# A three-layer block on one core: who issues the DMAs that turn an SWA pair's weights

## The chip, the cores and the metric

The kernel runs on one core of one Trainium2 chip. The metric is the device time in microseconds, the median of several executions. All data is 32-bit float; a product of two matrices is made of three TensorE products of high and low parts (see below).

## The reference, cut to what matters

The input x is 512 tokens of 2048 features. It passes an MLA attention layer, a sliding-window attention layer (SWA) and a third layer (stick-breaking attention and a gated recurrence), each with a projection in, a mixer, a gate and a projection out. The change touches the SWA layer:

```python
q, k, v, gate = split(rmsnorm(x) @ w_in)         # 32 query heads, 4 key/value heads, head size 64
q, k = rope(q), rope(k)                          # on the first 16 of 64 features
s = q_block @ k_window.T * 64 ** -0.5            # 128-query blocks, 256 keys (block before, own block)
s = where(0 <= query - key < 128, s, -1e30)
m = max(max(s), sink)
p = exp(s - m) / (sum(exp(s - m)) + exp(sink - m))
y = p @ v_window
x = x + (y * silu(gate)) @ w_out
```

## The kernel before, in words

The core's five engines run one instruction stream each: TensorE (the functions that end in `_T`), ScalarE (`_A`), VectorE (`_V`), GpSimd (`_G`) and SyncE (`sync_program` and the `_dmas` functions). They meet by semaphores: `q.did("turned")` counts a step up, `q.at("V.turned")` is the count to wait for. The order of every stream is written out by hand; there is no planner.

Every weight tile is 2048 x 128, loaded by SyncE into one of two `raw` buffers (1 MB) and treated in four pieces of 512 columns. ScalarE makes the high part of a piece (`hi`, line 604: a copy to fp32r), VectorE the low part (`lo`, line 612: the rest), TensorE does 4 x 3 matmuls on it (`multiply`, lines 638 to 640).

The SWA layer is a loop over 16 pairs of heads. Body i projects pair i (query tile, then gate tile, 48 matmuls each) and does the attention of pair i-1. Bodies 1 to 15 do both (`attn and proj`); body 16 has no projection and begins the output projection instead. In one body:

- TensorE: the scores of pair i-1 (16 matmuls, lines 1931 and 1932), the query tile's four pieces, the product of probabilities and values of pair i-2 (`pv_prev`, lines 1960 and 1962), the gate tile's four pieces.
- VectorE: `maxima` of the scores, the inverse sums, the low part of the gathered weights of pair i-2, then `turn_pair` for both heads (line 1898, a transpose inside 32 x 32 blocks, into `turned`; after the second one V.turned counts up). Then the rotary step on q (lines 2219 to 2224), the third low part of the gate tile, `q_lo0` and `q_lo1`, which wait for ScalarE's `q_hi0` and `q_hi1`, the gate tile's fourth low part, the sums for pair i-2 (line 2189), two elementwise steps, and the four low parts of the next query tile. The next body begins with the eviction of the gate (line 2180) and the maxima.
- ScalarE: the exponentials (line 2039), the normalisation (line 2060) with the gate tile's first and second high parts after one head each, a tanh, the third high part, `low_prev` (two copies out of PSUM, line 2067), the fourth high part, `q_hi0` and `q_hi1`, three high parts of the next query tile, `gathered_hi` (the high part of the gathered weights, 128 x 1792), and the fourth high part of the next query tile.
- SyncE: the loads of the next weight tiles, and after V.turned the 16 DMAs from `turned` to `gathered` (line 1161). These move 32 x 32 blocks between partition groups, 4 groups by 4 (QUADS = 4), and so finish the transpose that VectorE began. The next load of a weight tile stands behind them.

`gather_dmas(q, run, bands)` issues a DMA for each of the four destination column bands and each partition band in `bands`. Two constants, `SYNC_BANDS, SCALAR_BANDS = ((0, 1), (2, 3))` (line 46), halve the partition bands. In the MLA stage and in the third layer SyncE issues the first half and ScalarE the second; in the SWA stage SyncE issues all 16. `gathered_hi` waits for the semaphores of all DMAs of the pair, whoever issues them (lines 2071 and 2072).

Of the kernel before, what the change touches and what calls it, by code (L numbers as in the profile page):

```python
# [44 lines left out]
QUADS = P // Q32  # L45
SYNC_BANDS, SCALAR_BANDS = ((0, 1), (2, 3))
# [3 lines left out]
PAIR_SLOTS = 2 * 7 * Q32  # L50
# [316 lines left out]
def build(nc, x, positions, sinks, params, consts, w, out):  # L367
# [6 lines left out]
    with ExitStack() as ctx:  # L374
# [191 lines left out]
        def load_tile(eng, tile):  # L566
            if tile.has(RAW):
                eng.wait_ge(s_lo, tile.raw_free())
            for dst, src, s in weight_dmas(tile):
                eng.dma_start(dst, src).then_inc(s, 16)  # L570
# [20 lines left out]
        def hi(q, tile, p):  # L591

            if tile.at < 2:
                q.eng.wait_ge(s_first[tile.at][p], 16)
            elif p == 0:
                q.eng.wait_ge(s_raw[tile.slot], tile.loaded())
                if tile.phase == "mla" and tile.k == 1:
                    q.eng.wait_ge(s_ukv, lin(32, 32, tile.i))
            if tile.has(SPLIT // PIECES):
                q.eng.wait_ge(s_used, tile.slot_free(p))  # L600
            dst = split(w_hi, tile, p)
            if stacked(tile, p):
                dst = dst[:, :, 0:ROPE1]
            q.eng.activation(dst, raw_piece(tile, p), ACT.Copy).then_inc(s_hi, tile.ups(p))  # L604
# [60 lines left out]
        def loop(eng, a, b, step=1):  # L665
            return eng.Fori(a, b, step)
# [61 lines left out]
        def store_y(q, phase, body, tile_at):  # L728

            q.eng.wait_ge(*q.at("V.y" if phase == "mla" else "V.y_prev", body=body, phase=phase))  # L730
            q.eng.dma_start(y_dram[tile_at], (y_out if phase == "mla" else s_y)[:, 0, :]).then_inc(s_ystore, 16)

        def load_y(q, n, part):

            attention, units, last = BEFORE[n]
            stores = sum(BEFORE[m][1] - 1 for m in range(1, n)) + (4 * part + 4 if n < 3 and part < 3 else units - 1)
            q.eng.wait_ge(s_ystore, 16 + 16 * stores)
            q.eng.wait_ge(s_used, Tile(attention, units - 1, last).used(part))
            chunks = slice(4 * part, min(4 * part + 4, KC - 2 if n == 2 else KC - 1))
            q.eng.dma_start(y_whole[:, chunks, :], y_dram[chunks].rearrange("c p s -> p c s")).then_inc(s_yload[part], 16)  # L740

        def attention_dmas(q, phase, n):
            units, tiles = PHASES[phase][1:]

            def gather(i):
                q.eng.wait_ge(*q.at("V.turned", body=i, phase=phase))
                if phase == "mla":
                    gather_dmas(q, SLOTS, SYNC_BANDS)
                else:
                    gather_dmas(q, PAIR_SLOTS, range(QUADS))  # L750

            def unit(i, store, odd=None, turned=True):
                for k in range(tiles):
                    load_tile(q.eng, Tile(phase, i, k, odd))
                    if k == 0 and turned:
                        gather(i - 1)
                if store:
                    store_y(q, phase, i - 1, i - (2 if phase == "mla" else 3))
            unit(0, False, turned=False)
            unit(1, False, turned=False)  # L760
            if phase == "mla":
                with loop(q.eng, 2, units - 1, 2) as i:
                    unit(i, True, False)
                    unit(i + 1, True, True)
            else:
                unit(2, False)
                with loop(q.eng, 3, units) as i:
                    unit(i, True)
            load_tile(q.eng, Tile(f"out{n}", 0, 0))
            gather(units - 1)  # L770
            if phase == "mla":
                load_tile(q.eng, Tile(f"out{n}", 0, 1))
                for part in range(3):
                    load_y(q, n, part)
                store_y(q, phase, units - 1, units - 2)
            else:
                store_y(q, phase, units - 1, units - 3)
                q.eng.sem_inc(s_ystore, 16)
                load_y(q, n, 2)
            if n == 1:  # L780
                q.eng.wait_ge(*q.at("V.qn_lo", body=units - 1, phase=phase))
                q.eng.dma_start(s_pos_i, positions.to_broadcast([P, S])).then_inc(s_pos, 16)
                q.eng.wait_ge(*q.at("T.s0", body=units, phase=phase))
                q.eng.dma_start(s_sinks[:, 0, :], sinks.to_broadcast([P, H2])).then_inc(s_pos, 16)
# [371 lines left out]
        def gather_dmas(q, run, bands):  # L1156

            for half in range(2):
                for a in (2 * half, 2 * half + 1):
                    for k in bands:  # L1160
                        q.eng.dma_start(gathered[k * Q32:(k + 1) * Q32, a * run:(a + 1) * run],  # L1161
                                        turned[a * Q32:(a + 1) * Q32, k * run:(k + 1) * run]).then_inc(s_turned[half], 16)
# [860 lines left out]
        def swa_A(q, i, proj, attn, nxt):  # L2023
# [3 lines left out]
            def this_hi(p):  # L2027
                if proj:
                    hi(q, Tile("swa", i, 1), p)
# [33 lines left out]
            def low_prev(half):  # L2063

                if attn and (not isinstance(i, int) or i >= 2):
                    q.eng.wait_ge(*q.at(f"T.pv_prev{half}"))
                    q.eng.activation(s_y_low[0:HD2, half, :], PAIR_BANK[half][HD2:P, :], ACT.Copy).then_inc(*q.did(f"low_prev{half}"))
# [26 lines left out]
            if attn:  # L2094
                q.eng.wait_ge(*q.at("V.gate"))
                q.eng.activation(s_th[:, :], s_gate, ACT.Tanh, scale=0.5).then_inc(*q.did("tanh"))
            this_hi(2)
            low_prev(0)
            low_prev(1)
            this_hi(3)  # L2100
# [717 lines left out]
        @block.scalar  # L2818
        def _(eng):
            q = Program(eng, "A", sems, steps)  # L2820
            load_A(q)
            in_A(q)
            in_pairs(q, mla_A, Tile("out1", 0, 0))
            y_hi(q, 1, range(12, KC))
            output_A(q, 1)
            norm2_A(q)
            kv_A(q)
            pipelined(q, swa_A, "swa", Tile("out2", 0, 0))
            y_hi(q, 2, range(KC - 1, KC))
            output_A(q, 2)  # L2830
            norm3_A(q)
            pipelined(q, stick_A, "stick", Tile("out3", 0, 0))
            y_hi(q, 3, range(KC - 1, KC))
            output_A(q, 3)
# [75 lines left out]
```

## Time and profile before

| | |
|---|---|
| median of three runs | 2108.74 us (2108.37 to 2108.83) |
| the profiled execution | 2110.29 us, its span 2108.5 us |
| TensorE busy | 2089.3 us, 99% |
| VectorE busy | 1413.6 us, 67% |
| ScalarE busy | 995.6 us, 47% |
| granted TensorE clock, mean | 0.997 of full speed |
| the SWA loop, first score matmul of body 1 to that of body 16 | 771.19 to 1152.01 us |

Times in the profile are microseconds from the span's start. A group of instructions is named by line, engine, operation and "output<-input". An engine's busy share is an average over stages; in each stage only the wait that ends last counts. SPq, ACTq and DVEq are the instruction sequencers of SyncE, ScalarE and VectorE. A row's idle time in brackets is that of the engine before the row, and behind the arrow stands what ended it. Matmuls are pipelined, so the start of one to the start of the next (0.23 us for 512 columns) is what a matmul costs TensorE.

### The profile page before, as it was taken

To read this page: it belongs to the slowest core of one execution; us is meant where nothing else is said; L and a number is where in the kernel's file an instruction comes from. 1 tells how busy PE (TensorE), PEld (TensorE's weight loads), DVE (VectorE), ACT (ScalarE), POOL (GpSimd) and SP (SyncE) were. 2 spreads that over 40 slices of the span, in tenths; PEclk is the share of its full clock that TensorE was granted. 3 is DMA by queue.
4 is the path that set the end of the run, shared out by engine and by line. 5 is a ranking of instruction groups with operands and counts; after the bars stand their busy time and mean duration, and the time that the engine had idled before them with its cause. 6 is when DMAs were issued, how large, how long until landed. Compare 5 with 4: busy or idle time off the path is not lost. (4 is left out here: it accounts for less than half of the span.)

```text
span 2108.5 us, 30019 instructions
## 1 busy us (share of the span) xinstructions
PE 2089.3 (99%) x9716; PEld 1740.0 (83%) x9716; DVE 1413.6 (67%) x2575; ACT 995.6 (47%) x1925; POOL 191.5 (9%) x197
## 2 busy tenths in 40 slices
PE   9999999999999999999999899999999999999999
PEld 7888888888888888888887688888888888888887
DVE  6677777777633567888888533777777676769432
ACT  6444444444423446666666533544454545446221
POOL 0101111113101000100000122200000000003000
PEclk9999999999999999999999899999999999999999
DMA  7324444446634524444445534533434334345742
GB/s 231 95 80 115 115 113 110 109 110 184 191 80 123 169 72 122 127 126 132 132 133 159 176 100 118 168 104 80 118 92 134 82 103 114 103 114 155 214 115 70
DMA packets 405033, 262.88 MB, mean 125 GB/s; under 512 B 18928, under 2 KB 378096, under 8 KB 404976
## 3 DMA queue, kind: packets, MB, share of 16 engines
q1 hardware_dynamic: 393120, 251.27, 42.2%
q10 hardware_dynamic: 11856, 10.89, 1.9%
q8 instruction: 31, 0.51, 0.1%
q14 instruction: 26, 0.21, 0.0%
HBM read 210.07 MB, written 23.86 MB: 111 GB/s over the span
## 5 line engine op out<-in xcount | busy, mean ns | idle before, releaser
L638 PE MATMUL pp<-act_hi,w_hi 128*128 128x512 f32 x2304 | 905.4, 393 | 7.7 <-POOL act_lo L1545 3.3
L640 PE MATMUL pp<-act_hi,w_lo 128*128 128x512 f32 x2304 | 899.7, 390 | 0.0
L639 PE MATMUL pp<-act_lo,w_hi 128*128 128x512 f32 x2304 | 899.4, 390 | 0.0
L612 DVE TENSOR_TENSOR w_lo<-raw,w_hi 128x512 fp32r<-128x512 f32 x680 | 455.1, 701 | 357.9 <-ACT w_hi L604 357.0
L604 ACT ACTIVATE w_hi<-raw 128x512 fp32r<-128x512 f32 (+1 forms) x684 | 396.0, 622 | 460.8 <-PE pp L640 223.5
L638 PEld LDWEIGHTS pp<-act_hi,w_hi 128*128 128x128 f32 x2304 | 434.2, 188 | 101.5 <-DVE w_lo L612 6.5
L640 PEld LDWEIGHTS pp<-act_hi,w_lo 128*128 128x128 f32 x2304 | 433.8, 188 | 91.6
L639 PEld LDWEIGHTS pp<-act_lo,w_hi 128*128 128x128 f32 x2304 | 434.3, 189 | 87.0 <-issue 0.2
L657 POOL TENSOR_TENSOR pT_lo<-gathered,pT_hi 128x640 fp32r<-128x640 f32 x30 | 46.5, 1570 | 358.8 <-ACT pT_hi L653 358.8
L1314 ACT ACTIVATE prob<-ps,minus,q_scale 128x512 f32<-128x512 f32 (+1 forms) x64 | 39.0, 615 | 78.3 <-DVE minus L1394 78.3
L638 PE MATMUL ps<-act_hi,w_hi 128*128 128x512 f32 x176 | 69.3, 394 | 0.0
L640 PE MATMUL ps<-act_hi,w_lo 128*128 128x512 f32 x176 | 68.5, 389 | 0.0
L639 PE MATMUL ps<-act_lo,w_hi 128*128 128x512 f32 x176 | 68.5, 389 | 0.0
L2039 ACT ACTIVATE s_prob<-ps,s_minus 128x256 f32<-128x256 f32 x96 | 44.6, 471 | 42.7 <-DVE s_minus L2154 42.7
L1702 POOL TENSOR_TENSOR acc<-acc,square 128x512 f32<-128x512 f32 x30 | 41.1, 1371 | 252.6 <-ACT square L1628 251.8
L1545 POOL TENSOR_TENSOR act_lo<-y_lru,act_hi 128x512 fp32r<-128x512 f32 x7 | 11.1, 1619 | 560.5 <-ACT act_hi L1535 560.5
L653 ACT ACTIVATE s_pT_hi<-gathered 128x1792 fp32r<-128x1792 f32 x15 | 25.5, 1702 | 71.2 <-DMA gathered<-turned 71.2
L2060 ACT ACTIVATE s_prob<-s_prob,s_inv 128x256 f32<-128x256 f32 x128 | 54.3, 503 | 0.0
L2154 DVE CUSTOM_DVE_ANT_0 ps<-ps,s_con,s_sink 128x256 f32<-128x256 f32 x96 | 47.4, 549 | 3.2 <-DVEq L2151 3.2
L1898 DVE STREAM_TRANSPOSE turned<-s_prob 128x128 f32<-128x128 f32 (+1 forms) x60 | 35.1, 624 | 12.4 <-ACT s_prob L2060 12.4
L1679 DVE TENSOR_TENSOR xT<-pp,xT 128x512 f32 (+1 forms) x28 | 19.3, 689 | 32.1 <-PE pp L640 32.1
L639 PEld LDWEIGHTS ps<-act_lo,w_hi 128*128 128x128 f32 x176 | 33.0, 188 | 7.3 <-issue 0.5
(432 smaller groups left out, 2753.9 us busy)
## 6 DMA issues: line engine op xcount, KB each, us to landing
raw<-w_in SPq DMA_DIRECT2D x48, 1024.0 KB, 6.0
raw<-swa_w_in SPq DMA_DIRECT2D x36, 1024.0 KB, 5.9
raw<-mla_w_in SPq DMA_DIRECT2D x23, 1024.0 KB, 5.8
raw<-mla_w_out SPq DMA_DIRECT2D x16, 1024.0 KB, 6.8
raw<-w_out SPq DMA_DIRECT2D x16, 1024.0 KB, 6.8
raw<-swa_w_out SPq DMA_DIRECT2D x15, 1024.0 KB, 6.5
gathered<-turned SPq DMA_DIRECT2D x240, 56.0 KB, 2.0
x_feature_major<-xT SPq DMA_DIRECT2D x8, 1024.0 KB, 9.7
```

What stands on the lines that cost most here:

```text
L604: q.eng.activation(dst, raw_piece(tile, p), ACT.Copy).then_inc(s_hi, tile.ups(p))
L612: q.eng.tensor_tensor(dst, raw_piece(tile, p), high, ALU.subtract).then_inc(s_lo, tile.ups(p))
L638: q.eng.matmul(psum[:, :], wh, ah, start=start and n == 0, stop=False)
L639: q.eng.matmul(psum[:, :], wh, al, start=False, stop=False)
L640: last = q.eng.matmul(psum[:, :], wl, ah, start=False, stop=stop and n == PIECE // P - 1)
L657: q.eng.tensor_tensor(out, in_, hi_part.bitcast(F32), ALU.subtract).then_inc(*q.did(step))
L1314: q.eng.activation(prob[:, OFF[b]:OFF[b] + w_], SCORE[b][:, 0:w_], ACT.Exp, bias=minus[:, b:b + 1], scale=q_scale[:, b:b + 1], accum_out=t ...
L1702: q.eng.tensor_tensor(into, into, src[:, k, :], ALU.add).then_inc(*q.did(f"sum{f}{k}"))
L1898: m = q.eng.transpose(out_, in_)
L2039: q.eng.activation(s_prob[:, h, b * 2 * P:(b + 1) * 2 * P], BANKS[h][half][:, b % 2 * 2 * P:(b % 2 + 1) * 2 * P], ACT.Exp, bias=s_minus[:, ...
L2060: m = q.eng.activation(pr, pr, ACT.Identity, scale=s_inv[:, h, b:b + 1])
L2154: m = q.eng.tensor_tensor_reduce(scores, scores, sc("band")[:, b * 2 * P - half * 2 * P:(b + 1) * 2 * P - half * 2 * P], s_q_scale[:, b:b ...
```

## The change

SyncE issues eight of a pair's sixteen gather DMAs, those of partition bands 0 and 1. ScalarE waits for V.turned after the gate tile's third high part and issues the other eight, of bands 2 and 3. Nothing else is changed; the count that `gathered_hi` waits for is the same.

```diff
@@ attention_dmas (SyncE), gather(i) @@
                 if phase == "mla":
                     gather_dmas(q, SLOTS, SYNC_BANDS)
                 else:
-                    gather_dmas(q, PAIR_SLOTS, range(QUADS))
+                    gather_dmas(q, PAIR_SLOTS, SYNC_BANDS)
@@ swa_A (ScalarE) @@
                 q.eng.wait_ge(*q.at("V.gate"))
                 q.eng.activation(s_th[:, :], s_gate, ACT.Tanh, scale=0.5).then_inc(*q.did("tanh"))
             this_hi(2)
+            if attn and proj:
+                q.eng.wait_ge(*q.at("V.turned"))
+                gather_dmas(q, PAIR_SLOTS, SCALAR_BANDS)
             low_prev(0)
             low_prev(1)
             this_hi(3)
```

## Rows read from the trace of the kernel before

**Rows 1.** The page, busy time of each engine.
```profile
PE 2089.3 (99%) x9716; PEld 1740.0 (83%) x9716; DVE 1413.6 (67%) x2575; ACT 995.6 (47%) x1925; POOL 191.5 (9%) x197
```

**Rows 2.** Timeline of TensorE: start, duration, what; first score matmuls of bodies.
```profile
771.19 0.28 PE L1931 MATMUL ps<-pairk_hi,s_q_a 128*128 128x256 f32 x1
...
794.66 0.39 PE L640 MATMUL pp<-act_hi,w_lo 128*128 128x512 f32 x1
794.89 0.28 PE L1931 MATMUL ps<-pairk_hi,s_q_a 128*128 128x256 f32 x1
...
820.28 0.28 PE L1931 MATMUL ps<-pairk_hi,s_q_a 128*128 128x256 f32 x1
...
1126.30 0.28 PE L1931 MATMUL ps<-pairk_hi,s_q_a 128*128 128x256 f32 x1
...
1152.01 0.28 PE L1931 MATMUL ps<-pairk_hi,s_q_a 128*128 128x256 f32 x1
```

**Rows 3.** Waits: total, times, longest; weight loads 995 to 1145, TensorE 760 to 1210.
```profile
PEld pp L638 <- DVE w_lo L612: 1.6, 6, 0.3
...
PE pt L1943 <- DVE y_whole L2239: 3.7, 1, 3.7
```

**Rows 4.** Timeline of SyncE's issues, bodies 2 and 14.
```profile
808.57 10.02 SPq L1161 DMA_DIRECT2D gathered<-turned  x16
...
1116.78 10.03 SPq L1161 DMA_DIRECT2D gathered<-turned  x16
```

**Rows 5.** Timeline of ScalarE, body 14.
```profile
1117.14 1.08 ACT L2067 ACTIVATE s_y_low<-pt 64x512 f32<-64x512 f32 x2
1118.11 0.62 ACT L604 ACTIVATE w_hi<-raw 128x512 fp32r<-128x512 f32 x1
1120.13 0.63 ACT L653 ACTIVATE s_q_a<-s_q 64x512 fp32r<-64x512 f32 x1 [1.40 <-DVE s_q L2224]
...
1121.45 1.68 ACT L604 ACTIVATE w_hi<-raw 128x512 fp32r<-128x512 f32 x3
1128.28 1.70 ACT L653 ACTIVATE s_pT_hi<-gathered 128x1792 fp32r<-128x1792 f32 x1 [5.16 <-DMA gathered<-turned]
1129.88 0.61 ACT L604 ACTIVATE w_hi<-raw 128x512 fp32r<-128x512 f32 x1
```

**Rows 6.** Timeline of VectorE, bodies 1, 2 (first maxima) and 14.
```profile
772.54 0.55 DVE L2154 CUSTOM_DVE_ANT_0 ps<-ps,s_con,s_sink 128x256 f32<-128x256 f32 x1 [0.46 <-DVEq L2151]
...
798.18 0.55 DVE L2154 CUSTOM_DVE_ANT_0 ps<-ps,s_con,s_sink 128x256 f32<-128x256 f32 x1 [0.20 <-DVEq L2151]
...
1120.80 0.69 DVE L657 TENSOR_TENSOR s_q_a<-s_q,s_q_a 64x512 fp32r<-64x512 f32 x1 [0.16 <-ACT s_q_a L653]
...
1122.24 0.69 DVE L612 TENSOR_TENSOR w_lo<-raw,w_hi 128x512 fp32r<-128x512 f32 x1
...
1126.13 1.89 DVE L612 TENSOR_TENSOR w_lo<-raw,w_hi 128x512 fp32r<-128x512 f32 x3
1130.53 0.69 DVE L612 TENSOR_TENSOR w_lo<-raw,w_hi 128x512 fp32r<-128x512 f32 x1 [2.51 <-ACT w_hi L604]
1131.14 0.68 DVE L2180 TENSOR_TENSOR square<-pp,rstd 128x512 f32<-128x512 f32 x1
```

**Rows 7.** ScalarE's issues: timeline of two MLA bodies; all 176, min/median/max in ns.
```profile
293.24 5.03 ACTq L1161 DMA_DIRECT2D gathered<-turned  x8
298.38 1.68 ACT L604 ACTIVATE w_hi<-raw 128x512 fp32r<-128x512 f32 x3 [5.54 <-issue]
...
319.17 5.31 ACTq L1161 DMA_DIRECT2D gathered<-turned  x8
324.58 0.63 ACT L604 ACTIVATE w_hi<-raw 128x512 fp32r<-128x512 f32 x1 [6.33 <-PE pp L640]
...
L1161 ACTq DMA_DIRECT2D gathered<-turned x176: 514/614/875, 138.8 to 1883.3; - x176
```

**Rows 8.** Timeline of ScalarE, its first weight load of the tail.
```profile
1148.68 0.38 ACTq L570 DMA_DIRECT2D raw<-swa_w_out  x1
```

## The prediction

> **What bounds the kernel now.** I read the page first: TensorE is busy for 99% of the span [rows 1], so nothing gains unless TensorE's own waits shrink, and anything that makes TensorE wait costs in full. Then I read TensorE's timeline at the first score matmul of each SWA body [rows 2]. Body 2 starts at 794.89 and body 3 at 820.28, so a body of nothing but back-to-back matmuls lasts 25.39 us. Body 15 starts at 1126.30 and body 16 at 1152.01, which is 25.71. From 794.89 to 1152.01 are 14 bodies in 357.12 us; at 25.39 they would be 355.46, so TensorE waits only 1.66 us in the whole loop. The list of waits confirms it: six waits for w_lo of 1.6 us together in the last six bodies, and TensorE's larger ones, 3.7 for y_whole the longest, stand in the tail after the loop [rows 3].
>
> What makes those 0.26 us a body is a ring of work beside TensorE, and the timelines of SyncE, ScalarE and VectorE of one body show it [rows 4 to 6]. I count from I, the moment at which SyncE starts its first gather DMA (1116.78, released by VectorE's second transpose). SyncE issues 16 DMAs in 10.03 us, the last lands, and ScalarE starts the high part of the gathered weights at 1128.28 = I+11.50, having sat idle 5.16 us for it. The next weight piece's high part follows at 1129.88, its low part on VectorE at 1130.53 = I+13.75 (VectorE idle 2.51 before it), behind it the gate eviction at 1131.14, the maxima, the exponentials, the normalisation and the next transposes. That ring takes 25.64 us, a little more than TensorE's 25.39. The change cuts its DMA part.
>
> **Part 1, SyncE issues 8 instead of 16.** 10.03/16 = 0.63 us each, so SyncE is through at about I+5.0. With both queues at work the gathered tile should be complete at about I+7.4 instead of I+11.5 (last ScalarE issue near I+5.4, and some 2 us to landing, as in the list of the ScalarE issues [rows 7]). That removes the 5.16 us of ScalarE idle, if ScalarE gets there. By itself it is worth at most the 1.66 us that TensorE waits in the loop, and something in the tail. What is queued behind the gathers on SyncE gains nothing: the next gate tile's load also waits for the raw buffer, that is for the gate tile's fourth low part, which by the working below starts at I+9.0; it stood at about I+10.3 before, and its tile is read some 13 us later.
>
> **Part 2, ScalarE issues 8.** This is a new load on ScalarE's instruction stream, in the middle of its body. The MLA stage does the same thing with the same helper [rows 7]: 8 issues from 293.24 in 5.03 us, and the next ScalarE instruction at 298.38, 5.14 after the first issue, with 5.54 us of idle that is laid to issue and to no other engine; or 5.31 us from 319.17, and the next instruction at 324.58, 5.41 after. The 15 MLA bodies alternate between these two, and the 7 of the last stage lie at 5.1 to 5.5. So while DMAs are issued ScalarE computes nothing. I call this hold h and take 5.41, the longer of the two, because swa's DMAs are larger (56 KB each, against 40); 5.14 and 5.54 are the ends. The wait for V.turned costs nothing itself: SyncE's first issue, released by the same count, comes at 1116.78, and ScalarE's own high part before it is dispatched by then (low_prev follows at 1117.14).
>
> Queued behind the eight issues on ScalarE are low_prev (two copies), the gate tile's fourth high part, q_hi0, q_hi1, three high parts of the next tile, and only then the gathered high part. Before, against I [rows 5]: low_prev +0.36, fourth high part +1.33, q_hi0 +3.35 (it waited 1.40 for VectorE's s_q), the three next high parts, behind q_hi1, +4.67, gathered +11.50. After: low_prev +5.41; fourth high part +6.38 (0.97 later, as before); q_hi0 +6.90 (0.52 later, the cadence of the three high parts, (1.68-0.62)/2); the next high parts 1.32 later as before, +8.22; gathered +9.81 (three times 0.53, and by then it has landed); the next tile's last high part 1.60 later as before, +11.41.
>
> VectorE waits for q_hi0 [rows 6]: its q_lo0 came 0.67 after q_hi0, and the gate tile's fourth low part 1.44 after that, at 1122.24 = I+5.46. After: I+6.90+0.67+1.44 = I+9.01, 3.55 later. Two things hang on this.
>
> First, VectorE itself. From that low part to the first of the three low parts of the next tile pass 3.89 us (1122.24 to 1126.13), and the three take 3 x 0.61 (the cadence from 1130.53 to 1131.14), 5.72 in all. It is done at I+9.01+5.72 = I+14.73; the fourth next low part, which used to wait until I+13.75, now starts at I+14.73 without waiting. The 2.51 us of slack absorbs the larger part of the 3.55, and the ring becomes 0.98 us longer, not shorter: 25.64+0.98 = 26.62 us, against TensorE's 25.39. The bound passes from the DMA to VectorE's stream behind q_hi0.
>
> Second, TensorE needs the fourth low part for the last 12 matmuls of the body, which start 22.66 us after the body's first score matmul (25.39 less 2.73, twelve at just under the 0.23 that separates two matmuls in [rows 2]). I let them start 0.81 after the low part starts (its 0.69, and a tenth for the semaphore and the weight load), so at I+9.82, and the next body's scores begin 2.73 later.
>
> **The sum.** Body 1 has no previous pair (no low_prev, no sums), so it is not hurt and even gains: its gathered part no longer holds the gate eviction, which then waits for the scores. The maxima started 1.35 us after the scores in body 1 (771.19 and 772.54); in body 2 they came at 798.18 and would now come at 794.89+1.35 = 796.24, 1.94 earlier [rows 2, 6]. So I of body 2 is 808.57-1.94 = 806.63 [rows 4]. Its fourth low part serves TensorE at 816.45, before 794.89+22.66 = 817.55: no stall. Body 3: I = 833.25, ready 843.07 against 842.94, a stall of 0.1. From body 4 on each body stalls by 1.23. I of body 15 is 806.63+13 x 26.62 = 1152.69, and body 16's scores start at 1152.69+9.82+2.73 = 1165.24, against 1152.01: 13.2 us later.
>
> The tail behind it starts from the same low part: ScalarE's load of the first swa_w_out tile was issued at 1148.68, right after it [rows 8], and would come near 1162.4, 13.7 later. Against that, the gathers are out of the DMA queues when the tail's loads begin, which I put at half a microsecond gained. I take +13.2 in all. The profiled execution took 2110.29 us (span 2108.5), the median is 2108.74, 1.55 below it; the addition is the same on both: 2110.29+13.2 = 2123.5, and as a median 2121.9.
>
> With h = 5.14 the ring is 26.35, I of body 15 1149.2 and the loss 9.5; with 5.54 it is 26.75, and the loss 15.1. I allow 2 us more on either side for the tail. That gives 2116.5 to 2126.
>
> The Trainium skill weighs in from the other side. In "DMA: Bandwidth & Descriptors", section "Anatomy of one DMA", dispatch by the sequencer is put at about 50 ns of a DMA's fixed cost, and the section "Issuing engines are not separate DMA queues" says that starting DMAs on several engines saves only the sequencer's time, "usually small relative to the DMA itself". The former is written for GpSimd's path, and by it 8 issues would be an estimated 0.4 us and the change a small gain. The trace does not agree with it for ScalarE: 0.61 us for one issue, and 5.1 to 5.5 us of idle for eight.
>
> **The rivals.** (a) The hold is short or hidden: not slower. The shortest issue of ScalarE is 0.514 us [rows 7], 8 of them 4.1. The ring falls to 25.39 at h = 5.41-1.23 = 4.18; below this no body stalls, and the six small waits go. Then body 16 starts 1.66 earlier and its low part up to 5.8 earlier (the ring set by TensorE), which can take a few us of the tail's waits: 2103 to 2107, say 2105.5. The point that decides is h = 4.2. Against it: in none of 22 bodies is the hold under 5.09. For it: swa's ScalarE stream has more independent work than MLA's. (b) The hold is longer because 16 larger DMAs compete with the 1 MB weight loads: the longest single issue was 0.875 us, eight of them 7.0. The ring would be 28.21, I of body 15 1173.4, and body 16 1187.5, 35.5 later: 2144. Against it: SyncE's issues of the larger DMAs cost the same 0.63 alone. (c) The hold is real but shorter than in MLA, between 4.2 and 5.1, since an activation can still be in ScalarE's pipeline when the first DMA is issued. At h = 4.8 the ring is 26.01, I of body 15 1144.8, and body 16 starts at 1144.8+9.21+2.73 = 1156.7, 4.7 later: 2113.4, and 2110 to 2118 with the tail.
>
> **Chances.** Forecast 0.80, (a) 0.07, (b) 0.05, (c) 0.08. The range runs from 2114 to 2128, so that it takes in the larger half of (c). A difference of 0.2% (4.2 us) is about what a measurement of this kernel can tell from none. (a) gives 1.4 to 5.7 below the median, mostly within that: faster 0.03, same 0.07, slower 0.90.
>
> **What would show it.** The period of I, and of the score matmuls, in bodies 4 to 15: 26.6 us, 25.4 in rival (a). TensorE waits for w_lo of about 1.2 us in twelve bodies, at the gate tile's fourth piece. ScalarE idle of 5 us before low_prev, put down to issue. No wait of the gathered high part for DMA, nor of VectorE's fourth low part for ScalarE; instead VectorE waits some 3.5 us for q_hi0. I would be wrong if ScalarE ran low_prev between the issues, or if another instruction than q_hi0 held VectorE.

## The result, and the profile after

The changed kernel takes 2117.96 us, median of five runs (2117.13 to 2118.72), against 2108.46 for the kernel before (five runs, the three above among them): ratio 1.0044, 95% interval 1.0032 to 1.0056. It is slower by 9.5 us. The profiled execution took 2117.59 us, its span 2115.8, which is 7.3 more than the profiled one of before; the latter lay 1.8 above its median of 2108.46 and the former 0.4 below its own, so 9.5 by the medians and 7.3 by the profiled pair are the same result.

The sum had two parts, the loop and the tail, and TensorE's timeline separates them. The rows are the restart of TensorE at the gate tile's fourth piece of body 14, and the first score matmuls of bodies 15 and 16, in the changed kernel.

```profile
1135.67 0.50 PE L638 MATMUL pp<-act_hi,w_hi 128*128 128x512 f32 x1 [0.91 <-DVE w_lo L612]
...
1138.52 0.28 PE L1931 MATMUL ps<-pairk_hi,s_q_a 128*128 128x256 f32 x1
...
1165.11 0.28 PE L1931 MATMUL ps<-pairk_hi,s_q_a 128*128 128x256 f32 x1
```

Body 16 starts at 1165.11, 13.1 us later than in [rows 2]. From there to the end of the span are 950.7 us; before they were 2108.5-1152.01 = 956.5. So the loop lost 13.1 and the tail gave back 5.8 (in the profiled pair; if the loop lost the same in the other executions, the medians' 9.5 leave some 3.6). What these 5.8 are made of is shown under "The tail" below.

The ring beside TensorE, in body 14 of the changed kernel. ScalarE (the answer to [rows 5]):

```profile
1125.91 5.32 ACTq L1161 DMA_DIRECT2D gathered<-turned  x8
1131.34 1.08 ACT L2067 ACTIVATE s_y_low<-pt 64x512 f32<-64x512 f32 x2 [5.10 <-issue]
1132.31 0.62 ACT L604 ACTIVATE w_hi<-raw 128x512 fp32r<-128x512 f32 x1
1132.83 0.62 ACT L653 ACTIVATE s_q_a<-s_q 64x512 fp32r<-64x512 f32 x1
...
1134.14 1.67 ACT L604 ACTIVATE w_hi<-raw 128x512 fp32r<-128x512 f32 x3
1135.71 1.69 ACT L653 ACTIVATE s_pT_hi<-gathered 128x1792 fp32r<-128x1792 f32 x1
```

VectorE (the answer to [rows 6]); its line numbers behind the edit are three higher:

```profile
1133.49 0.69 DVE L657 TENSOR_TENSOR s_q_a<-s_q,s_q_a 64x512 fp32r<-64x512 f32 x1 [3.72 <-ACT s_q_a L653]
...
1134.92 0.69 DVE L612 TENSOR_TENSOR w_lo<-raw,w_hi 128x512 fp32r<-128x512 f32 x1
...
1138.82 2.49 DVE L612 TENSOR_TENSOR w_lo<-raw,w_hi 128x512 fp32r<-128x512 f32 x4
1141.23 0.68 DVE L2183 TENSOR_TENSOR square<-pp,rstd 128x512 f32<-128x512 f32 x1
```

SyncE (the answer to [rows 4]):

```profile
1125.90 4.98 SPq L1161 DMA_DIRECT2D gathered<-turned  x8
1135.79 0.38 SPq L570 DMA_DIRECT2D raw<-swa_w_in  x1
```

Read them against I = 1125.90. ScalarE issues for 5.32 us and starts low_prev at I+5.44, after 5.10 us of idle laid to issue. q_hi0 comes at I+6.93, the fourth low part at I+9.02. The gathered high part no longer waits for a DMA (its row has no bracket, and starts at I+9.81). VectorE's idle has moved: 2.51 us ahead of the fourth next low part are gone (the four low parts are one run, x4), and 3.72 us stand ahead of q_lo0. TensorE waits 0.91 us at the gate tile's fourth piece; the list of waits has twelve of them:

```profile
PE pp L638 <- DVE w_lo L612: 10.8, 12, 0.9
```

Their 10.8 us are the matmul side; the weight loads' own list has 15.9 us for the same twelve, 1.32 each. The period is longer by a little less, 1.20 (26.59 against 25.39). The tail: SyncE's gathers of body 15 and ScalarE, before

```profile
1142.50 10.33 SPq L1161 DMA_DIRECT2D gathered<-turned  x16
...
1149.19 4.55 ACTq L740 DMA_DIRECT2D y_whole<-y_feature_major  x1
...
1164.85 2.19 ACT L1535 ACTIVATE act_hi<-y_whole 128x512 fp32r<-128x512 f32 x4 [5.58 <-DMA y_whole<-y_feature_major]
```

and after

```profile
1152.58 4.96 SPq L1161 DMA_DIRECT2D gathered<-turned  x8
...
1158.26 0.41 ACTq L740 DMA_DIRECT2D y_whole<-y_feature_major  x1
...
1162.23 0.38 ACTq L570 DMA_DIRECT2D raw<-swa_w_out  x1
...
1162.74 1.55 ACTq L740 DMA_DIRECT2D y_whole<-y_feature_major  x1
...
1173.06 2.19 ACT L1535 ACTIVATE act_hi<-y_whole 128x512 fp32r<-128x512 f32 x4 [4.02 <-DMA y_whole<-y_feature_major]
```

The second load of y_whole is issued 13.55 us later but used only 8.21 later: from issue to use it takes 10.3 us instead of 15.7, and its issue holds ScalarE 1.55 us instead of 4.55.

### The profile page after: what moved, and what is told of

The parts are those of the page before. It is cut to its first block and busy times, and to the rows that moved or that the text cites. A ratio compares the mean times of both kernels' runs of the same rounds, so it can differ in the third digit from the quotient of the medians.

```text
span 2115.8 us, 30032 instructions
## 1 busy us (share of the span) xinstructions
PE 2087.2 (99%) x9716; PEld 1735.0 (82%) x9716; DVE 1412.3 (67%) x2575; ACT 992.0 (47%) x1925; POOL 195.3 (9%) x197
## 5 line engine op out<-in xcount | busy, mean ns | idle before, releaser
L1545 POOL TENSOR_TENSOR act_lo<-y_lru,act_hi 128x512 fp32r<-128x512 f32 x7 | 11.1, 1617 | 560.6 <-ACT act_hi L1535 560.6
L2067 ACT ACTIVATE s_y_low<-pt 64x512 f32<-64x512 f32 x30 | 16.2, 589 | 71.2 <-issue 71.2
L657 DVE TENSOR_TENSOR s_q_a<-s_q,s_q_a 64x512 fp32r<-64x512 f32 x16 | 11.0, 685 | 52.6 <-ACT s_q_a L653 52.6
```

The source lines that it names most:

```text
L657: q.eng.tensor_tensor(out, in_, hi_part.bitcast(F32), ALU.subtract).then_inc(*q.did(step))
```

## The experiments

The theory (H): ScalarE's hold, through q_hi0, delays VectorE, and the ring that this makes exceeds TensorE's 25.39 us a body only once the hold passes 4.2 us. Its rivals: the second queue or its contention makes the loss (S), and a cost in proportion to ScalarE's DMAs wherever they stand (R, M). Every kernel was timed beside the kernel before, whose median was 2109.20 to 2109.75 us beside the variants (2108.46 beside the change), so rows are compared by their ratios. Body 16's start, the period and the rest of the span are from the trace.

| variant | median us | ratio to before, 95% | period, late bodies | body 16 starts | rest of the span |
|---|---|---|---|---|---|
| the change (8 on ScalarE) | 2117.96 | 1.0032 to 1.0056 | 26.59 | 1165.11 | 950.7 |
| 8, behind q_hi1 | 2139.90 | 1.0126 to 1.0157 | 27.5 | 1179.20 | 959.8 |
| 8, behind q_hi1, weight load later | 2108.66 | 0.9986 to 1.0006 | 25.39 | 1150.43 | 956.2 |
| 4, behind q_hi1 | 2106.44 | 0.9975 to 0.9993 | 25.39 | 1150.76 | 955.0 |
| 4, at the change's place | 2105.16 | 0.9971 to 0.9989 | 25.39 | 1150.67 | 952.7 |
| 6, at the change's place | 2102.65 | 0.9954 to 0.9978 | 25.39 | 1149.85 | 949.5 |
| 6, once more | 2103.24 | 0.9958 to 0.9982 | 25.39 | 1150.08 | 950.5 |
| 7, at the change's place | 2109.42 | 0.9991 to 1.0009 | 25.95 | 1156.39 | 951.4 |
| 10, at the change's place | 2137.04 | 1.0115 to 1.0146 | 27.9 | 1183.44 | 950.5 |
| 8, body 15 alone | 2108.16 | 0.9986 to 1.0004 | 25.66 | 1155.57 | 950.8 |
| 8, bodies 1 to 14 | 2120.54 | 1.0038 to 1.0066 | 26.60 | 1164.40 | 954.3 |
| 28 copies on ScalarE, no DMA | 2108.98 | 0.9988 to 1.0007 | 25.66 | 1152.65 | 954.6 |
| 53 copies on ScalarE, no DMA | 2121.96 | 1.0044 to 1.0074 | 26.56 | 1166.29 | 953.9 |

**The place.** Against the change, the block moves behind q_hi1:

```diff
             this_hi(2)
-            if attn and proj:
-                q.eng.wait_ge(*q.at("V.turned"))
-                gather_dmas(q, PAIR_SLOTS, SCALAR_BANDS)
...
                 copy_hi(q, s_q_b[HD2:P, :], s_q[HD2:P, :], "q_hi1", rest=not attn)
+            if attn and proj:
+                q.eng.wait_ge(*q.at("V.turned"))
+                gather_dmas(q, PAIR_SLOTS, SCALAR_BANDS)
```

> ScalarE issues the same eight DMAs, but behind q_hi1 instead of ahead of low_prev. Theory H (the hold of ScalarE delays q_hi0, through it VectorE's stream, and nothing else matters): q_hi0 is back at I+3.35, ScalarE issues from about I+3.6 to I+8.9, the gathered tile lands near I+10.9, its high part starts there and VectorE's fourth next low part at I+13.1. The ring is some 24.9 us, TensorE's own 25.39 sets the period, no body waits for w_lo: 11.5 to 13 us faster than the change in the loop, body 16's scores near 1150.4, and the time at or a few us under the kernel before (2104 to 2108). Rival R (ScalarE issuing eight DMAs costs its stream 5.4 us wherever they stand, or two queues at once disturb the rest): the period stays above 26 us and the time within 3 us of the change's, 2118.

Neither was right: 2139.9. Its trace, ScalarE and then SyncE, in body 13 (I = 1114.75):

```profile
1118.11 0.63 ACT L653 ACTIVATE s_q_a<-s_q 64x512 fp32r<-64x512 f32 x1 [1.40 <-DVE s_q L2227]
1118.23 0.51 ACTq L1161 DMA_DIRECT2D gathered<-turned  x1
1118.77 0.63 ACT L653 ACTIVATE s_q_b<-s_q 64x512 fp32r<-64x512 f32 x1
1118.77 4.47 ACTq L1161 DMA_DIRECT2D gathered<-turned  x7
1123.44 1.68 ACT L604 ACTIVATE w_hi<-raw 128x512 fp32r<-128x512 f32 x3 [4.04 <-issue]
1128.06 1.70 ACT L653 ACTIVATE s_pT_hi<-gathered 128x1792 fp32r<-128x1792 f32 x1 [2.95 <-DMA gathered<-turned]
```

```profile
1114.75 4.96 SPq L1161 DMA_DIRECT2D gathered<-turned  x8
1121.08 0.38 SPq L570 DMA_DIRECT2D raw<-swa_w_in  x1
```

q_hi0 is back at I+3.36, as expected. But SyncE, free early, issues the 1 MB weight load at I+6.3, in the middle of ScalarE's gathers, and the gathered tile is used at I+13.3, not I+10.9. The three gathers that ScalarE issues behind that load take 4.9 to 5.8 us to land in bodies 2 to 14; the five ahead of it, like every gather of the change, take at most 2.3. The ring then goes through the landing again, and is longer than it ever was. Two later kernels tested that reading. One issues four DMAs there and leaves twelve to SyncE, so that all are out before the weight load (shown against the kernel just described):

```diff
-                    gather_dmas(q, PAIR_SLOTS, SYNC_BANDS)
+                    gather_dmas(q, PAIR_SLOTS, (0, 1, 2))
...
-                gather_dmas(q, PAIR_SLOTS, SCALAR_BANDS)
+                gather_dmas(q, PAIR_SLOTS, (3,))
```

> ScalarE issues four, behind q_hi1; SyncE twelve. The variant with eight there had a ring of 27.5 us. Theory L (its last DMAs were issued after SyncE's 1 MB weight load and landed behind it, 5.8 us instead of 2): here ScalarE's issues run from I+3.5 to I+6.2, before that load, all land by I+9.6, period 25.39, median 2103 to 2107. Rival M (DMAs behind q_hi1 hold the next tile's high parts, and that makes the loss, half of it with four): a period near 26.4 and 2118 to 2124.

The other keeps all eight behind q_hi1 and issues the store of y ahead of the weight load (the store waits for V.y_prev):

```diff
                 for k in range(tiles):
+                    if k == 1 and store and phase == "swa":
+                        store_y(q, phase, i - 1, i - 3)
                     load_tile(q.eng, Tile(phase, i, k, odd))
...
-                if store:
-                    store_y(q, phase, i - 1, i - (2 if phase == "mla" else 3))
+                if store and phase == "mla":
+                    store_y(q, phase, i - 1, i - 2)
```

> As the variant with eight DMAs behind q_hi1 (period 27.5, the last gathers landing up to 5.8 us after issue), but SyncE issues its 1 MB weight load behind the store of y, at about I+9.3 instead of I+6.3, so that all of ScalarE's gathers are issued ahead of it. Theory L (the weight load ahead of them makes them land late): they land near I+11, ring 25.0, period 25.4, body 16's scores near 1151, median 2108 to 2113 with the longer tail of that variant. Rival M (ScalarE's issues behind q_hi1 are late or hold the high parts of the next tile): the period stays above 26.5, above 2128.

Both came out as theory L has it: 2106.44 and 2108.66, no loss in the loop. In the second, body 14:

```profile
1111.54 4.95 SPq L1163 DMA_DIRECT2D gathered<-turned  x8
1121.18 0.38 SPq L731 DMA_DIRECT2D y_feature_major<-s_y  x1
1121.81 0.39 SPq L570 DMA_DIRECT2D raw<-swa_w_in  x1
```

The weight load stands at I+10.3, and ScalarE's gathered high part started at 1122.65, I+11.1, without a wait. Moving that load by 4 us, behind the gathers and the store, is worth 31 us, 28.8 of them in the loop. It also answers rivals R and M: ScalarE issues all eight here, and the loop loses nothing.

**The number at the change's place.** Four (the diff above, without the move), six, seven and ten; for these `gather_dmas` got a list of extra and missing pairs of bands.

> ScalarE issues four DMAs (band 3) at the place of the change, SyncE twelve. Theory H: the hold is 2.7 us, q_hi0 comes at I+4.2, 0.85 later than before the change, the gathered tile lands near I+9.5, VectorE's three next low parts are done at I+12.0: the ring is 23.9 us, under TensorE's 25.39, no loss in the loop and the six small waits gone; 2104 to 2108. Rival R (the loss goes with the number of ScalarE's DMAs): half the loss, a period of 26.0 and about 2113.

> ScalarE issues six at the place of the change, SyncE ten. Theory H: hold 4.15 us, right at the point from which a body stalls: period 25.4, body 16's scores at 1150.4 to 1151, the tail a little shorter than with four: span 2102 to 2104, median 2103.5 to 2106, no slower than with four. Rival S or a cost in proportion to the number: 6.5 us slower than with four, near 2112.

> The variant with six DMAs on ScalarE once more, beside other runs of the kernel before: if its gain is real it comes out 5 to 8 us faster than before (2101 to 2105); if it was the luck of the tail, within 3 us of the variant with four, 2105.

> ScalarE issues seven at the place of the change, SyncE nine. The hold is 4.75 to 4.8 us, 0.6 over the break-even. Theory H (a threshold near 4.2 and slope one beyond it): period 26.0, body 16's scores at 1156 to 1157.5, six to seven us later than with six DMAs, median 2108 to 2111. Rival: no threshold but a cost that grows with each DMA would have shown in four and six already; if seven lies with six (period 25.4), the break-even is put wrong.

> ScalarE issues ten of the sixteen at the place of the change, SyncE six. Theory H (the ring is TensorE's 25.39 until ScalarE's hold passes 4.2 us, and grows by the hold from there): hold 6.7 us, ring 27.9, body 16's scores near 1183.3, span near 2134, median 2135 to 2137. Rival S (what costs is that the work is split over two queues, not how much ScalarE issues): as the change, 2118.

The holds, from SyncE's first issue to ScalarE's low_prev, are 4.14 us for six, 4.79 for seven, 5.44 for eight and 6.70 for ten; the periods 25.39, 25.95, 26.59 and 27.87 (ten as the mean from body 4 to body 16; single bodies alternate between 26.3 and 29.5). From seven to ten the slope is 1.92/1.91, one to one, and the line meets 25.39 at 4.2 us. Six, just under it:

```profile
1110.97 4.03 ACTq L1161 DMA_DIRECT2D gathered<-turned  x6
1115.11 1.08 ACT L2067 ACTIVATE s_y_low<-pt 64x512 f32<-64x512 f32 x2 [3.81 <-DVE s_q L2227]
1116.09 0.62 ACT L604 ACTIVATE w_hi<-raw 128x512 fp32r<-128x512 f32 x1
1116.61 0.62 ACT L653 ACTIVATE s_q_a<-s_q 64x512 fp32r<-64x512 f32 x1
...
1117.91 1.68 ACT L604 ACTIVATE w_hi<-raw 128x512 fp32r<-128x512 f32 x3
1119.49 1.69 ACT L653 ACTIVATE s_pT_hi<-gathered 128x1792 fp32r<-128x1792 f32 x1
```

No row waits for a DMA, and TensorE loses nothing. It beat the kernel before twice, on different chips, 2102.65 against 2109.75 and 2103.24 against 2109.20, by 7.1 and 6.0 us. Mind the bracket: 3.81 us of idle are ascribed to VectorE's s_q, though the engine was issuing.

**The hold without DMAs.** The kernel before, SyncE issuing all sixteen, and in the place of ScalarE's DMAs small copies (first 28 of 128 x 8, then 53 of 128 x 4):

```diff
             this_hi(2)
+            if attn and proj:
+                q.eng.wait_ge(*q.at("V.turned"))
+                for n in range(53):
+                    q.eng.activation(below[:, 4 * n:4 * n + 4], s_con[:, 0:4], ACT.Copy)
             low_prev(0)
```

> The kernel before, SyncE issuing all sixteen, with 28 copies of 128 x 8 to an unused place on ScalarE where the change puts its DMAs (behind V.turned): some 28 x 0.19 = 5.3 us in which ScalarE does no work of the body, and no DMA of its own. Theory H (the hold alone makes the loss): period 26.5 to 26.6 as in the change, body 16's scores near 1165, the tail as in the kernel before or as in the variant with body 15 unchanged, 2119 to 2122. Rival S (the second queue or its contention makes the loss): the period stays at 25.4 to 25.7, 2108 to 2110.

> As the variant with copies in place of DMAs, but 53 copies of 128 x 4: the 28 of before took 2.87 us, 0.10 each, a hold of 2.9 us, under the 4.2 from which a body stalls, and the period had stayed as in the kernel before. 53 make 5.4 us, the hold of the change. SyncE still issues all sixteen. Theory H: ring 26.6, body 16's scores at 1164 to 1166, median 2118 to 2122. Rival S (the second queue makes the loss, and a busy ScalarE does not): period 25.7, 2108 to 2110.

The first did not test what it should: a copy took 0.10 us, not 0.19, and a hold of 2.9 us costs nothing, which theory H allows and rival S as well. The second decides:

```profile
1127.25 5.15 ACT L2101 ACTIVATE below<-s_con 128x4 f32<-128x4 f32 x53
1132.41 1.08 ACT L2067 ACTIVATE s_y_low<-pt 64x512 f32<-64x512 f32 x2
```

With the same hold and no second queue, the period is 26.56 and body 16 starts at 1166.29. The loop's whole loss is reproduced (body 16 starts 14.3 us later than in [rows 2]; in the change it was 13.1); rival S falls.

**The tail.** Once with the change in body 15 alone, once in all bodies but that one (`ends` is true in body 15):

```diff
-            if attn and proj:
+            if attn and proj and ends:        # the other kernel: not ends
                 q.eng.wait_ge(*q.at("V.turned"))
                 gather_dmas(q, PAIR_SLOTS, SCALAR_BANDS)
```

> The change in body 15 alone; bodies 1 to 14 as before. Loop: the fourth low part of body 15 is ready at 1142.5+9.8 = 1152.3 instead of 1148.9, so body 16's scores start 3.0 later than before, at 1155.1. Tail, which was 5.8 us shorter in the change's trace: theory G (the 16 gather DMAs of body 15 on SyncE's queue stand in the way of the tail's loads, and eight on each queue don't): the tail is about as short as with the change, net 2.8 us faster than before, near 2105.5 and the y_whole load of 10 to 11 us instead of 15.6. Theory C (the tail only hides lateness that the bodies before have piled up): the tail is as long as before, net +3, near 2111.5.

> The change in bodies 1 to 14, body 15 as before. Loop: I of body 15 stays at 1152.6, its own stall goes, body 16's scores near 1164, 12 us later than before. Theory G: the tail is as long as before the change, net +12, near 2120.4, slower than the change itself. Theory C: the tail is 5 to 6 us shorter all the same, net +6, near 2115.

Theory G holds in its direction. With the change in body 15 alone the loop ends 3.6 us later than in [rows 2], and the rest of the span is 950.8 us, as with the whole change; with it everywhere else, the rest is 954.3. The second load of y_whole tells them apart, 10.3 us from issue to use in the first:

```profile
1153.20 1.50 ACTq L740 DMA_DIRECT2D y_whole<-y_feature_major  x1
1163.46 2.19 ACT L1535 ACTIVATE act_hi<-y_whole 128x512 fp32r<-128x512 f32 x4 [3.91 <-DMA y_whole<-y_feature_major]
```

and 15.4 in the second:

```profile
1159.73 4.08 ACTq L740 DMA_DIRECT2D y_whole<-y_feature_major  x1
1175.09 2.19 ACT L1535 ACTIVATE act_hi<-y_whole 128x512 fp32r<-128x512 f32 x4 [5.14 <-DMA y_whole<-y_feature_major]
```

By the totals G's sizes were too large: -1.1 us for the first, 2108.16, where -2.8 was expected, and the interval includes no change; +11.3 for the second, 2120.54, where +12 was.

The traces show why, if one counts from I of body 15 and not from body 16's start. The kernel with 53 copies on ScalarE tells most, since it holds ScalarE as the change does and leaves all sixteen gathers to SyncE:

```profile
1153.67 10.30 SPq L1161 DMA_DIRECT2D gathered<-turned  x16
...
1163.89 2.38 ACTq L740 DMA_DIRECT2D y_whole<-y_feature_major  x1
...
1176.61 2.19 ACT L1535 ACTIVATE act_hi<-y_whole 128x512 fp32r<-128x512 f32 x4 [5.72 <-DMA y_whole<-y_feature_major]
```

| variant | body 15's gathers | I of body 15 | second y_whole load issued | used | body 16 starts | span ends |
|---|---|---|---|---|---|---|
| before | 16 on SyncE | 1142.50 | I+6.7 | I+22.4 | I+9.5 | I+966.0 |
| 8, bodies 1 to 14 | 16 on SyncE | 1153.04 | I+6.7 | I+22.0 | I+11.4 | I+965.7 |
| 28 copies | 16 on SyncE | 1142.35 | I+7.9 | I+22.4 | I+10.3 | I+964.9 |
| 53 copies | 16 on SyncE | 1153.67 | I+10.2 | I+22.9 | I+12.6 | I+966.6 |
| the change | 8 and 8 | 1152.58 | I+10.2 | I+20.5 | I+12.5 | I+963.2 |
| 8, body 15 alone | 8 and 8 | 1143.00 | I+10.2 | I+20.5 | I+12.6 | I+963.4 |

"Used" is the start of ScalarE's act_hi that waited for the load. Each row is one execution, and that of the kernel before lay 1.8 us above its median, so the last column is good to a microsecond or two. With sixteen on SyncE the load is used at about I+22.4, whether it is issued at I+6.7 or at I+10.2: a part of the 15.7 us from issue to use was only an early issue. Splitting the gathers eight and eight brings the use forward by some 2 us (with six on ScalarE it is at I+21.0 and 21.1, with four at I+23.4) and the end by 1.5 to 3.4. The 5.8 us of the profiled pair are therefore, in this pair, 2.8 of the gathers and 3.0 by which body 16 starts later behind I (12.5 against 9.5). These 3.0 are a part of the loop's loss that the tail doesn't feel, since it waits for loads that hang on I; in that, theory C is right too. In the kernel before, ten of body 15's gathers take 5.0 to 6.9 us to land beside the tail's loads; in the change none takes over 2.3.

## Why the prediction was right, and where its size was off

The direction, the mechanism and the loop's numbers held. **The hold**: 5.41 us taken, 5.44 measured. **The ring**: 26.62 taken, 26.59 measured, through the three instructions named (q_hi0, q_lo0, the fourth low part at I+9.01, measured I+9.02). **The bound's passing** from the DMA to VectorE's stream: both waits that were to vanish are gone, the one that was to come is there, 3.72 us. **TensorE's stall**: first in body 3 (a period of 25.68; 0.1 was worked out, 0.3 measured), then 1.2 in each of twelve bodies, at the gate tile's fourth piece. **Body 16's start**: 1165.24 worked out, 1165.11 measured; two small errors cancel in it, since TensorE starts 0.75 us behind the low part's start and not 0.81, and the next scores come 2.85 later and not 2.73. That the break-even is at 4.2 us was an inference from the rows of one body; six, seven, eight and ten DMAs show it.

The step that was mis-sized is the tail. I put "the gathers are out of the DMA queues when the tail's loads begin" at half a microsecond, and let the tail start with body 16. The whole term measured 5.8 in the profiled pair and some 3.6 by the medians, and that is nearly all of the difference between 2121.9 and 2117.96. By the profiled pair the gathers' part is 2.8 us; the other 3.0 is that the tail hangs on I of body 15, which came 10.1 us later, and not on body 16's start, which came 13.1 later (10.1 less 2.8 is the 7.3 of the two spans). The row that would have told it was there before the change: the load of y_whole, 15.7 us from issue to use where the page has medians of 6 to 11 for the other million-byte loads, with its own issue held for 4.55 us. I had read the time of the issue [rows 8] and not what stood in front of the load. The issue itself came when I said, 13.55 us later against 13.7; it was the landing that did not follow it. Why the loads land 2 us sooner when the same bytes move in another order, no run separates.

The total alone would have shown little. 2117.96 lies in the 2110 to 2118 of rival (c) too, and it is all but what a hold of 5.14 would have given (2108.74+9.5 = 2118.2): there a hold taken too short and the tail put too long would have cancelled by luck. That the eight issues would take the longer of the two MLA holds was right, but that the DMAs' size is the reason is not shown. It is the period, 26.59, that tells the forecast from these. Two sums of the prediction are a little off by their own terms: the lower bound is 2108.74+9.5-2 = 2116.2, not 2116.5, and (a)'s 2107 is 1.7 below the median, not 1.4. Neither changes the range.

The rivals: (a) fell at eight DMAs, but it is the case at six, where the hold is 4.14. (c) is the case at seven: 2109.42, no difference from before, since the tail gives back what the loop loses. (b) did not occur: single issues took up to 0.885 us, the eight together never over 5.33.

The idea of the change was sound, its share was not: the wait that it removed cost TensorE 1.7 us in the loop and the tail some more, and moving DMAs to ScalarE wins that back only while ScalarE's hold fits into the slack around q_hi0.

## What to carry to other kernels

A DMA's issue is work on the engine that issues it, and splitting a batch over two engines pays up to the slack of the second: work out the break-even from the consumer that waits longest behind it (here low_prev's 0.36 us behind I, 1.40 of ScalarE's own wait and 2.51 of VectorE's, less the 0.25 by which the ring was longer than TensorE's body: an estimate of 4.0, where the line through seven and ten meets 25.39 at 4.2), and give it as many DMAs as fit, not half. When a queue is relieved, look at what it will issue next and earlier: a large load that slips ahead of small transfers on another queue can cost more than the whole batch.

## What the runs showed of the hardware that I had not expected

- Gathers of 56 KB that ScalarE issues just behind a 1 MB load of SyncE's take 4.9 to 5.8 us to land, against 1.9 to 2.3 without one, though they are on another queue. It holds the other way round too: in the kernel before, SyncE's last ten gathers of body 15, beside ScalarE's loads, take 5.0 to 6.9. The Trainium skill has the reason beside it, in "DMA: Bandwidth & Descriptors", section "Issuing engines are not separate DMA queues": all run on the same 16 DMA engines and interleave. The landing times agree with that; the rows here do not show the sharing itself.
- Copies of 128 x 4 and of 128 x 8 last 0.19 and 0.20 us each in ScalarE's records, but follow each other at 0.10: 53 of them took 5.15 us.
- A DMA behind an activation in the program can be issued before that activation has begun: in the variant behind q_hi1 the first issue starts at 1118.23, 0.12 after q_hi0 and 0.54 before q_hi1, though it stands behind both. What stands behind the issues was held: the next high parts start at 1123.44, 0.20 after the last issue ends.
